# Values and forget gate of the second stage computed token-major, ahead of the attention units

## What is computed

```python
kvf = rmsnorm(x, kv_norm) @ w_kv                      # 1024 -> 768 keys, 768 values, 12 gates
k_sh, v_sh = kvf[..., :768], kvf[..., 768:1536]       # 12 heads of 64
log_f_cum = jnp.cumsum(jax.nn.log_sigmoid(kvf[..., 1536:] + b_f), axis=1)
h = rmsnorm(x, b_norm1)
z = h @ b_w_q                                         # 768 token queries, 256 memory queries
tok = forgetting_attention(q, k_sh, v_sh, log_f_cum)  # causal softmax, bias c[t] - c[s]
mem_o = memory_attention(q_mem, mem, ...)             # 4 heads over 256 memory rows
x = x + concat([tok, mem_o]) @ b_w_out
```

## Time and profile before

| | |
|---|---|
| median of 3 runs | 1510.24 us (1509.49 to 1512.92) |
| the profiled execution | 1509.61 us, of which the traced span is 1507.8 us |
| granted TensorE clock, mean | 0.998 |
| PE matmul busy in the span | 1464.9 us, 97% |
| DVE, ACT busy | 962.2 us (64%), 673.2 us (45%) |
| stage of the change | 555.68 us (first gate product) to 785.32 us (first block that needs unit 7) |

### The profile page before, as it was taken

How to read it: one execution, slowest core, us unless ns; L and a number is a source line. 1 busy time by engine, 2 the same in 40 slices (tenths; PEclk the granted TensorE clock), 3 DMA queues, 4 the chain that set the end, 5 groups by cost and what they waited for, 6 DMA issues and landing times.

```text
span 1507.8 us, 20197 instructions
## 1 busy us (share of the span) xinstructions
PE 1464.9 (97%) x7144; PEld 1158.9 (77%) x7144; DVE 962.2 (64%) x1504; ACT 673.2 (45%) x1106; POOL 37.5 (2%) x75
## 2 busy tenths in 40 slices
PE   7999999999999999999999999999999999999988
PEld 7966778888888887666667888888888767777767
DVE  5655667777766656555446777777677665566562
ACT  6444444444442234444344444444332455665651
POOL 0000000000001110000000000000111000000000
PEclk9999999999999999999999999999999999999999
DMA  6331222222247722111122222223676311112121
GB/s 228 124 101 70 80 88 97 97 97 97 97 139 235 243 80 85 56 57 43 57 85 67 101 97 95 97 90 110 220 239 213 129 57 56 57 57 70 57 98 56
DMA packets 43189, 159.18 MB, mean 106 GB/s; under 512 B 4917, under 2 KB 5429, under 8 KB 43129
## 3 DMA queue, kind: packets, MB, share of 16 engines
q1 hardware_dynamic: 33768, 126.40, 24.7%
q0 software_dynamic: 8208, 29.89, 5.9%
q10 hardware_dynamic: 1152, 2.10, 0.4%
HBM read 156.27 MB, written 2.10 MB: 105 GB/s over the span
## 4 chain that ended last, share of the span: by engine, by line
PE 84%; DVE 6%; ACT 6%; issue 3%; DMA 1%; SPq 0%; POOL 0%; ACTq 0%; DVEq 0%; POOLq 0%
PE ps L363 17%; PE ps L364 17%; PE ps L365 17%; PE ps L379 5%; PE ps L381 4%; PE ps L380 4%; PE ps L466 2%; PE ps L539 2%; PE ps L1762 1%; PE ps L1764 1%; PE ps L1763 1%; PE ps L527 1%; DVE wl L297 1%; PE ps L1882 1%; PE ps L1636 1%
## 5 line engine op out<-in xcount | busy, mean ns | idle before, releaser
L291 ACT CAST wh<-raw 128x1024 fp32r<-128x1024 f32 (+3 forms) x208 | 228.5, 1098 | 256.5 <-PE ps L365 216.2
L297 DVE TENSOR_TENSOR wl<-raw,wh 128x1024 fp32r<-128x1024 f32 (+3 forms) x208 | 266.0, 1279 | 115.0 <-ACT wh L291 114.8
L363 PE MATMUL ps<-xh,wh 128*128 128x512 f32 x720 | 281.2, 390 | 1.6 <-DVE wl L297 1.6
L365 PE MATMUL ps<-xh,wl 128*128 128x512 f32 x720 | 280.1, 389 | 0.0
L364 PE MATMUL ps<-xl,wh 128*128 128x512 f32 x720 | 280.1, 389 | 0.0
L363 PEld LDWEIGHTS ps<-xh,wh 128*128 128x128 f32 x720 | 135.2, 188 | 31.1 <-DVE wl L297 2.5
L364 PEld LDWEIGHTS ps<-xl,wh 128*128 128x128 f32 x720 | 135.2, 188 | 28.3 <-issue 0.5
L365 PEld LDWEIGHTS ps<-xh,wl 128*128 128x128 f32 x720 | 135.2, 188 | 28.0
L379 PE MATMUL ps<-xh,wh 128*128 128x512 f32 x344 | 146.2, 425 | 2.6 <-DVE wl L297 2.6
L363 PE MATMUL ps<-hth,wh 128*128 128x512 f32 x352 | 136.9, 389 | 0.0
L364 PE MATMUL ps<-htl,wh 128*128 128x512 f32 x352 | 136.9, 389 | 0.0
(11 more groups left out here) (303 smaller groups left out, 2357.1 us busy)
## 6 DMA issues: line engine op xcount, KB each, us to landing
raw<-w_a_f SPq DMA_DIRECT2D x44, 512.0 KB, 3.2
raw<-w_b_f SPq DMA_DIRECT2D x44, 512.0 KB, 3.2
row<-w_c_rows POOLq DMA_DIRECT2D x32, 512.0 KB, 4.6
row<-w_ada_rows POOLq DMA_DIRECT2D x24, 512.0 KB, 4.8
raw<-w_a_f SPq DMA_DIRECT2D x16, 704.0 KB, 4.1
raw<-w_b_f SPq DMA_DIRECT2D x16, 704.0 KB, 4.2
raw<-w_b_pair SPq DMA_DIRECT2D x18, 512.0 KB, 3.2
raw<-w_front SPq DMA_DIRECT2D x16, 512.0 KB, 3.2
```

The source lines that it names most:

```text
L291: nc.scalar.copy(wh[:, s, :width], raw[:, s, :width]).then_inc(w_hi, 1)
L297: nc.vector.tensor_tensor(wl[:, s, :width], raw[:, s, :width], wh[:, s, :width].bitcast(F32), ALU.subtract).then_inc(w_lo, 1)
L363: nc.tensor.matmul(dst, a, h(k), start=(k == 0), stop=False)
L365: mm = nc.tensor.matmul(dst, b, h(k), start=False, stop=(k == total - 1))
```

## The change

- The `gate` job, the two `b_qm` jobs and the six value jobs leave their places. In place of gate and values stand two groups of products with the tokens on the output's partitions: `kv_values(0)` makes value columns 0 to 383, `kv_values(1)` columns 384 to 767 and the 12 gates (396 columns). A group is 8 x 4 x 3 = 96 products. Activations are now the stationary operand. Its weights come in six wider chunks (`b_v`; 1152, 1152, 768, then 1188, 1188, 792 columns).
- Inside group 0, before its last eighth: per-token sums (`columns`) and the norm sum. Inside group 1, likewise: the replication.
- ACT empties group 0 into `vnb`, DVE group 1, each with a per-token factor; four small transposes bring the gates back.
- The other 14 jobs (`b_in`) come in a new order: 2 before the units, 12 in them. `turn_pair`, `vtb`, `pair_values` go.
- Memory unit 1 moves from place 3 to place 4. `FILL` becomes 2, 2, 2, 2, 1, 2, 1, 0. In unit 6 the second half of the steps does 8 early `b_out` blocks, unit 7 does the other 20, two in each step; none is left behind it.

```diff
-          ("gate", 1, 1), ("b_qm", 2, 2), ("b_pair", 18, 18), ("b_out", 8, 8), ("b_f1", 44, 44),
+          ("b_v", 6, 0), ("b_in", 14, 14), ("b_out", 8, 8), ("b_f1", 44, 44),
...
+BSETS = ((0, 3), (3, 3), (6, 2))
+NG = 12
+B_IN = [("m", 0), ("k", 0), ("q", 0), ("k", 1), ("q", 1), ("k", 2), ("q", 2), ("m", 1),
+        ("k", 3), ("q", 3), ("k", 4), ("q", 4), ("k", 5), ("q", 5)]
+B_FIRST = 2
...
-        UNITS = [("mb", 0), ("fx", 0), ("fx", 1), ("mb", 1), ("fx", 2), ("fx", 3), ("fx", 4), ("fx", 5)]
-        FILL = [3, 3, 2, 2, 2, 3, 3, 0]
+        UNITS = [("mb", 0), ("fx", 0), ("fx", 1), ("fx", 2), ("mb", 1), ("fx", 3), ("fx", 4), ("fx", 5)]
+        FILL = [2, 2, 2, 2, 1, 2, 1, 0]
+        PARTS = [2, 2, 2, 2, 1, 2, 2, 0]
...
# ACT, ahead of the units
-                if k == 6:
-                    norm_root(act, 3, rbc[:, :])
...
+            value_hi(2)
+            value_hi(3)
+            act.wait_ge(c_sum, 3)
+            nc.scalar.activation(sm[:, 52:56], ob[:, 256:260], ACT.Sqrt, bias=eps, scale=1.0 / D).then_inc(c_root, 1)
+            norm_root(act, 3, rbc[:, :])
+            table(EXP_LN_SET)
+            act.wait_ge(c_rec, 3)
+            for b in range(TT):
+                if b == 0:
+                    act.wait_ge(w_used, C0["b_v"] + 3)
+                nc.scalar.activation(vnb[:, b, :VW], bbank[0][b][:, :VW], ACT.Copy, scale=sm[:, 52 + b:53 + b]).then_inc(b_vn, 1)
+            for i in range(4, 7):
+                value_hi(i)
...
-                    if name == "fx" and t == 0:
-                        pair_values(it)
...
# DVE, ahead of the units
+            value_lo(2)
+            value_lo(3)
+            dve.wait_ge(c_root, 3)
+            nc.vector.reciprocal(sm[:, 52:56], sm[:, 52:56]).then_inc(c_rec, 1)
+            norm_factor(dve, 3, rbc[:, :])
+            for i in range(4, 7):
+                value_lo(i)
+            for b in range(TT):
+                r = sm[:, 52 + b:53 + b]
+                if b < TT - 1:
+                    dve.wait_ge(b_done, b + 1)
+                else:
+                    dve.wait_ge(w_used, C0["b_v"] + 6)
+                nc.vector.tensor_scalar(vnb[:, b, VW:], bbank[1][b][:, :VW], r, None, ALU.mult)
+                nc.vector.tensor_scalar(gl[:, b, :], bbank[1][b][:, VW:VW + NG], r, None, ALU.mult).then_inc(b_vg, 1)
+            value_lo(7)
...
+            for i in range(B_FIRST):
+                project(i)
+                split(i)
...
# PE
+            def kv_values(g, mid):
+                for i, (k0, nk) in enumerate(BSETS):
+                    n, w = C0["b_v"] + 3 * g + i, VW + NG * g
+                    s = n % 2
+                    pe.wait_ge(w_lo, n + 1)
+                    for k in range(k0, k0 + nk):
+                        if g == 0:
+                            pe.wait_ge(x_lo, X0["kv"] + k + 1)
+                        if k == KD - 1:
+                            mid()
+                        a, b = wh[:, s, (k - k0) * w:(k - k0 + 1) * w], wl[:, s, (k - k0) * w:(k - k0 + 1) * w]
+                        for m in range(TT):
+                            hi, lo = xh[:, k, m * P:(m + 1) * P], xl[:, k, m * P:(m + 1) * P]
+                            dst = bbank[g][m][:, :w]
+                            nc.tensor.matmul(dst, hi, a, start=(k == 0), stop=False)
+                            nc.tensor.matmul(dst, hi, b, start=False, stop=False)
+                            mm = nc.tensor.matmul(dst, lo, a, start=False, stop=(k == KD - 1))
...
+            kv_values(0, kv_sums)
+            pe.wait_ge(po_free, J0["b_v"])
+            pe.wait_ge(c_root, 3)
+            pe.wait_ge(s_root, 4)
+            kv_values(1, replicate)
...
+            pe.wait_ge(b_vg, 2)
+            pe.wait_ge(x_lo, X0["b_q"] + 8)
+            b_blocks(0, 0, KD)
+            pe.wait_ge(b_vg, 4)
+            for b in range(TT):
+                mm = nc.tensor.transpose(st[0:NG, b * P:(b + 1) * P], gl[:, b, :], ident)
+            mm.then_inc(g_turn, 1)
+            b_blocks(1, 0, KD)
...
-                pe.wait_ge(mix_lo, (MIXB + (7 if k < 7 else 8)) if stage == "b_out" else ...)
+                pe.wait_ge(mix_lo, MIXB + max(6, k + 1) if stage == "b_out" else ...)
...
-                    if UNITS[u][0] == "fx" and t == 0:
-                        turn_pair(UNITS[u][1])
-                    if u == 7 and t >= 1:
-                        for i in range(25 * (t - 1) // (PE_STEPS - 1), 25 * t // (PE_STEPS - 1)):
+                        if j < n:
+                            b_blocks(first + j, a, e)
+                        else:
+                            for i in range(a, e):
+                                out_block("b_out", *B_EARLY[i])
+                    if u == 7:
+                        for i in range(8 + 2 * t, 10 + 2 * t):
                             out_block("b_out", *B_EARLY[i])
...
-            for i in range(25, 28):
-                out_block("b_out", *B_EARLY[i])
```

More of the change, by code:

```diff
@@ L642, in f @@
                 for j in range(jobs[1]):
[L643 removed]
+                    if end_step(j, jobs[2]) + 1 == t:
                         project(jobs[0] + j)
@@ L745, in _ @@
             load_stage("a_f2", 4, 4)
[L746 to L749, removed]
+            for i in range(6):
+                load_b_v(i)
+            for i in range(14):
+                load_one("b_in", i)
             load_stage("b_out", 2, 4)
@@ L938, in forget_act @@
                     nc.scalar.activation(fg[0:12, 2, :], fg[0:12, 2, :], ACT.Ln, bias=kf[0:12, K_ONE:K_ONE + 1]).then_inc(c_l, 1)
-            rounds(act, "b_qm", 2, 1, split_hi, lambda it, l, nxt: nxt())
             def project(i):
[L943 to L948, removed]
+                split_hi(act, C0["b_in"] + i + 2, C0["b_in"] + i + 2)
+            project(0)
+            project(1)
             for u, (name, it) in enumerate(UNITS):
@@ new lines, in kv_sums, with replicate @@
+            def kv_sums():
+                columns(ob[:, 256:260], acc, TT)
+                nc.tensor.matmul(st[:, :], ones, acc[:, :], start=True, stop=True).then_inc(s_sum, 1)
+            def replicate():
+                pe.wait_ge(b_vn, 4)
+                pe.wait_ge(diag, KD)
+                for h in range(2):
+                    nc.tensor.matmul(lg[h][:, :], ones, rowt[0][:, h * S:(h + 1) * S], start=True, stop=True).then_inc(rep_ps, 1)
+            kv_values(0, kv_sums)
+            pe.wait_ge(po_free, J0["b_v"])
@@ new lines, in _, with b_blocks @@
+            pe.wait_ge(c_root, 3)
+            pe.wait_ge(s_root, 4)
+            kv_values(1, replicate)
+            XB = (lambda k: xbh[:, k, :]), (lambda k: xbl[:, k, :])
+            def b_blocks(i, first, end):
+                blocks(pe, "b_in", i, *((X, XL) if B_IN[i][0] == "k" else XB), first, end)
+            pe.wait_ge(b_vg, 2)
[4 more added lines that the diff above has]
+                mm = nc.tensor.transpose(st[0:NG, b * P:(b + 1) * P], gl[:, b, :], ident)
@@ L1747, in out_block @@
                     pe.wait_ge(w_lo, n + 1)
-                    if j == 2 and stage == "b_out":
-                        pe.wait_ge(b_vn, 6)
                     if j == 3 and stage == "b_out":
@@ L2030, in layout @@
         "w_a_f2": ffn_out(a["a_ffn_out"][0]),
-        "w_gate": pack(chunk(gate, 0)),
-        "w_b_qm": pack(*(chunk(bq, 6 + l) for l in range(2))),
-        "w_b_pair": pack(*(chunk(w, c) for it in range(6) for w, c in ((kv, it), (bq, it), (kv, 6 + it)))),
+        "w_b_v": pack(*(np.pad(wide(v, 0, VW + NG * g, k0, nk), ((0, 0), (0, 3 * (VW + NG) - nk * (VW + NG * g))))
+                        for g, v in enumerate((kv[:, TOKW:TOKW + VW], kv[:, TOKW + VW:2 * TOKW + NG])) for k0, nk in BSETS)),
+        "w_b_in": pack(*(chunk(kv if kind == "k" else bq, c + (6 if kind == "m" else 0)) for kind, c in B_IN)),
         "w_b_out": pack(*(chunk(a["b_w_out"][0], j) for j in range(KD))),
```

121 lines of the change are left out of this document (52 added, 69 removed).

## The result

The changed kernel is slower: the ratio of its time to that of the kernel before is 1.003, with a 95% interval of 1.0023 to 1.0037 (medians of 18 runs each, 1514.11 and 1509.13 us). The forecast was 1512.8, 2.6 us above before; by the ratio 4.5 are measured (3.5 to 5.6), and the medians are 5.0 apart. Of the chances, "slower" had 0.40 and "within 0.2%" 0.48.

A forecast was written before the change was run, and what follows sets the result against it. The prediction took PE to bound the stage except in the windows, where DVE's queue does. Its terms, 49.6 + 20.6 + 114.2 + 17.7 + 30.15, gave 232.25 against 229.64, 2.6 longer, hence 1512.8 us; range 1507.0 to 1516.0.

The forecast's parts named there:

- Front: Stage start to unit 0's first logits: two value groups, sums, replication, two jobs, gate transposes, one block; 49.6 against old 21.67.
- the third rival: A value chunk's split is late and PE waits in group 1, or the forget chain costs 2.8: +5.5, 1515.7, chance 0.14.
- Unit 0: First unit: second logits at 3.3, 15.87 for the rest, 1.4 of waiting from the forget chain; 20.6, old 23.22.
- The window: Unit start, first to second logits, set by DVE's queue before the maxima: 4.28 in token units, 4.63 in the memory unit.
- Token units: Units 1, 2, 3, 5 and 6, two jobs each: 22.84 apiece, sum 114.2, nothing gained from the vanished `turn_pair`.
- Unit 4: Memory unit with one job: start of 4.63 with one block, tiles 3.5 + 3.5, last 6.1; 17.7 (16.4 to 18.7).
- tile 1: In unit 4, the tile behind the second logits, values waiting for ACT's copies: 3.5.
- Unit 7 and tail: Last unit with its tail: 3.5, 4.9, 7.35, 7.05, 5.85, then 1.5 waiting for `mixl`; 30.15, old 35.56.
- PE's work against its waits: Whole stage: PE's work falls by about 7, waits grow by 9 to 10, as fewer blocks stand in windows and tiles.
- The windows did not close up: Rival: second logits follow PE's own work in token units, 3.1 instead of 4.28; -4.4, 1505.8, chance 0.12.
- the short units did not wait less: Rival: unit 0's chain hidden, unit 4 at its lower bound, unit 7 near it; about -0.7, 1509.5, chance 0.14.

The follow-up runs named there:

- late leftover: Changed kernel, DVE's evacuation and split of a job ending in a unit's last steps moved behind the next unit's first two maxima: 0.9973, median 1505.36 us.
- the wait filled: Changed kernel with 24 transposes of the identity, read by nobody, added at the start of unit 4: 1.0016, median 1511.86 us.
- the turn back: Changed kernel with four transposes of the identity added at step 0 of units 1, 2, 3, 5 and 6, where `turn_pair` stood: 1.0031.
- the blocks behind unit 7: Changed kernel with three of unit 7's 20 output blocks put behind it, the other 17 spread over its steps: 1.0024.
- the early blocks: Changed kernel with unit 4's eight blocks moved forward among its steps, three instead of one in the first two steps: 1.002.
- the counts swapped: Changed kernel with the fill of units 3 and 4 exchanged, one job in unit 3 and two in unit 4: 1.004.
- the reordering alone: Kernel before, with evacuation and split of a job ending in a unit's last steps moved behind the next unit's first two maxima: 0.9998.

## Why the prediction was right or wrong

- **Front**, 49.6 forecast, 49.78 measured. Group 0 lasts 18.41 (forecast 18.4), group 1 19.12 (576.03 to 595.15; forecast 18.8 and 0.15 of waiting). The 396 columns cost 0.180 a product and not the interpolated 0.178. The prediction's remark that the trace has both widths 5% above the formula of the Trainium skill (TensorE: Matmul & The Clock Gate, Back-to-back issue gap) is right for 512 columns only (0.2267 against 0.2158); 384 columns stand 7% above it (0.1733 against 0.1625). The sum does not use it. PE waits for no split in either group, so the third rival did not happen.
- **Unit 0**, 20.6 forecast, 20.19 measured. The window took 3.23 for 3.3, the rest 16.96 for 17.3. Of the rest, 1.1 are more than unit 3's 15.87, where I took 1.4 from a reckoning of queue orders; 0.76 of it is one wait, for the turned tile at the last values.
- **Token units**, 22.84 forecast, 22.83 to 22.90 measured from first logits to first logits, with waits of 1.30 to 1.40 at the second logits. This is the core of the prediction, and the late leftover shows its cause, DVE's queue: in windows of unchanged length the block and the turn that left became waiting.
- **Unit 4**, 17.7 forecast within 16.4 to 18.7, 19.85 measured. The order of events was right in all its parts: the window 4.62 for 4.63, tile 2 3.40 for 3.5, the last 6.02 for 6.1. The term that was mis-sized is tile 1, 3.5 forecast and 5.81 measured. I took the clock of 1.00 in the earlier trace rows as given, while my own sum put a wait of about 3 into the unit (the old 1.66 and two blocks of 0.69). With the wait filled the unit lasts 17.54. This one term, 2.3 too small, is as large as the whole error of the sum, 234.46 against 232.25; the other differences (front 0.2, unit 0 -0.4, unit 7 0.2) cancel.
- **Unit 7 and tail**, 30.15 forecast, 30.38 measured: the window 3.59 for 3.5, tile 1 5.19 for 4.9, tile 2 7.27 for 7.35 (with a wait of 1.82), the rest 12.89 for 12.9, and the wait for `mixl` 1.44 for 1.5.
- **PE's work against its waits**, forecast 7 less against 9 to 10 more. Measured are 8.6 more of waiting. The work is 3.8 less by the clock on the wall, about 6.1 less with the 2.3 of the slow tile taken out. The forecast's 7 had 1.2 of waiting in the front in it; work alone it was 5.8 less, and waits alone some 8.4 more, close to the measured 6.1 and 8.6.
- **The rivals.** The windows did not close up, and the short units did not wait less, apart from 0.4 in unit 0. The measured 4.5 stands at the upper end of the forecast's own range, 0.8 to 4.5, because of a fourth case that was not on the list. It is also above the 3.0 that the prediction took as the limit of "within", which it held more likely (0.48) than "slower" (0.40). With the clock held by useless work the kernel is 2.4 above before (1.0016), near the forecast 2.6: the sum was right but for the clock. That the measured time lies within the range all the same is luck: the price of the clock was in none of the bounds, and the other terms left room for it.

## What to carry to other kernels

Work taken off the bounding engine pays only where that engine's own work sets the pace: find the stretches whose length another engine's queue fixes, and reorder that queue together with the cut. Here the cut alone cost 0.3%, the reordering alone gave nothing measurable (0.9998), and the two together gain 0.27%. And when a sum puts a wait of some microseconds into TensorE's stream, search the trace for such a wait anywhere in the kernel and read the granted clock behind it, before you price what follows at full speed. Do it in more than one profiled execution if you can: the twelve here do not agree on waits under 3 us.

## What the runs showed of the hardware that was not expected

The granted clock fell behind the wait of 3.38 to 3.40 of the first layer in all twelve profiles (to 0.50 in windows that lie wholly in a fall), and behind 3.02 and 3.03 in all three that have it (unit 4 of the changed kernel, and of the ones with the turn back and with the blocks behind unit 7). Below that the profiles differ: it fell behind 2.64 to 2.94 in the third layer in seven of twelve, and behind 1.75 to 1.77 in the first layer in four of twelve. It did not behind 2.70 and 1.82 in units 3 and 7, nor behind 1.66 in the kernel before and with the early blocks; it did behind 1.66 with the counts swapped, and not when the wait of 2.70 in the unit ahead had been filled. The price differs between executions too: unit 4 lasted 19.85 in one profile and 18.86 in two others in which it ran the same instructions but for their start in time. The windows of the kernel with the three blocks behind unit 7 show a difference that goes with it:

```profile
698.00:700.00 2.00, 0.54 (x4) 0.30 (x4) 1.63 (x7) 1.02 (x4) 0.00 (x0) 1.00 0.48 119
700.00:702.00 2.00, 2.00 (x10) 1.55 (x8) 1.42 (x6) 1.18 (x5) 0.00 (x0) 0.64 0.36 143
```

Its second logits are at 699.46 and the clock falls only after them, behind the wait and not in it, so the first work behind the wait still runs at full speed: the logits take 0.70 where they took 1.23 in the changed kernel, whose clock fell inside the wait. The Trainium skill (TensorE: Matmul & The Clock Gate, "What's actually happening") says that one kernel starts with different numbers of slow matmuls from run to run. No run here looks at the start of a kernel; in its middle these traces show the like, 19.85 and 18.86 for the same unit. What exactly brings the clock down, and when, these runs leave open.
